# An expert layer of a two-block transformer in 18 steps for 24: lanes of 64, 32 and 32 slots, dealt from the experts' counts

## The chip, the cores and the metric

One core of a Trainium2 chip runs the whole program in one launch. The metric is the device time in microseconds of one execution, the median of several runs; lower is better.

## The reference, cut to what matters

Two transformer blocks over 512 tokens of 1024 features, all in f32. The first has two kinds of attention, and then a mixture of 32 experts in 4 groups of 8: a router takes the best group of each token and the best 2 experts in it, so 1024 token-expert pairs are computed:

```python
for g in range(N_GROUPS):
    a = jnp.einsum('td,edf->tef', t, w_gate[sl])
    u = jnp.einsum('td,edf->tef', t, w_up[sl])
    hid = jax.nn.silu(a) * u * combine[:, g, :, None]
    y = y + jnp.einsum('tef,efd->td', hid, w_down[sl])
```

An expert has w_gate and w_up (1024 x 256 each) and w_down (256 x 1024), 1 MB each. `combine` is zero but for a token's two experts. The second block (two more attentions, two dense FFNs of 4096) is not touched by the change.

## The kernel before, in words

Each engine has its own instruction stream, and the streams meet at semaphores. Tiles keep the features on the 128 partitions, tokens on the free axis, but for the expert layer, which works on gathered rows.

**The router.** After the first block's attention, TensorE computes the router's logits and turns the normed tokens, which ACT writes to a table in HBM (`tokens_normed`). DVE picks groups and experts (L3044 to L3066), TensorE counts for each token-expert pair its place among the pairs of that expert, and each expert's total (L1777 to L1786, group "rank"). From these DVE works out the position of each pair among all slots (L3079 to L3103: `whole` rounds, a scan sums the extra blocks, the positions are added up under the one-hot choice), splits it into step and slot (L3106, L3108), and builds one-hot matrices (L3117, L3121). TensorE multiplies them into a table of slots (L1793), and DVE writes from it the token of each slot, the row of its output and its weight (`slot_tok`, `slot_y`, `slot_w`, L3130 to L3135), and the experts of the extra blocks with a flag for used (`extra_exp`, L3137, L3138). DVE instructions that need the one ahead are joined by `link`, a semaphore that DVE waits for itself.

**The steps.** There are 24 steps of 128 slots in two halves (`HALF` = 64). Steps 0 to 15 in `COLUMN`'s numbering are fixed: the halves belong to experts 2c and 2c+1. Eight more steps take what goes over 64 in an expert, in blocks of 64 of one expert each; `COLUMN` puts them between the fixed ones, after steps 2, 4, 6, 8, 10, 11, 12 and 13. Step b does:

- POOL gathers the 128 token rows with an indirect DMA (L1248; three buffers), and slots without a token are left out;
- TensorE turns them (L1805, eight transposes, "moe_T"), DVE adds a shift on the way out of PSUM (L3146);
- `gate_up` (L1821, "moe_GU"): for each of 8 slices of features, one product for each half, with 64 columns of tokens as the stationary operand and 512 columns of that expert's w_gate and w_up moving. The two halves write to partitions 0 to 63 and 64 to 127 of one PSUM bank;
- ACT takes the silu (L2499), DVE multiplies with the other half and the slot's weight (L3160);
- `turn_hidden` (L1831) and `down` (L1847, "moe_D"): two transposes, then four products for each half, to two banks;
- ACT and DVE copy the banks out (L2189, L2710), POOL scatters the rows to `y_dram` (L1257).

TensorE's order (`moe_schedule`) is turn_hidden(b), gate_up(b+1), turn_tokens(b+2), down(b). A product in f32 shows as two records in the trace. L1805, L1831 have the full 128 columns as stationary operand, L1821 and L1847 have 64.

**The weights.** SP's queue issues all loads in the order of its code. Expert weights have five places (`ESLOTS`), one per half-step: half n goes to place n % 5. SP loads halves 0 and 1, then 2, 3, 4 during the end of the attention and the router; after gate_up(b) it loads w_gate and w_up of the halves that take these places (L1037, L1039), after down(b-1) w_down of theirs (L1044). A fixed half has an address known when the program is written. For an extra one SP reads the expert and the flag from `extra_exp` into registers (`value_load`), and the DMA is skipped where the flag is 0. Behind the layer, the next stage's weights (L1113) wait for the third last step's down products.

```python
            for b in range(STEPS - 1):
                sp.wait_ge(mm_done, done(G[("moe_GU", b)]))
                for n in range(2 * b + ESLOTS, min(2 * b + ESLOTS + 2, 2 * STEPS)):
                    load_gate_up(n)
```

Most of the rest of the program is TensorE's: the dense products of the two FFNs and the projections, as three products of split halves (L1425 to L1427).

Of the kernel before, what the change touches and what calls it, by code (L numbers as in the profile page):

```python
# [40 lines left out]
MAGIC = float(1.5 * 2 ** 23)  # L41
PI = 3.1415925
# [15 lines left out]
PAIRS = NE // 2  # L58
EXTRA = 8
STEPS = PAIRS + EXTRA  # L60


COLUMN = []
for _b in range(PAIRS):
    COLUMN.append(_b)
    if _b in (2, 4, 6, 8, 10, 11, 12, 13):
        COLUMN.append(PAIRS + len([c for c in COLUMN if c >= PAIRS]))
COLUMN += [PAIRS + n for n in range(len([c for c in COLUMN if c >= PAIRS]), EXTRA)]
ESLOTS = 5
TOKEN_BUFS = 3  # L70
# [269 lines left out]
def two_block_kernel(nc, a, out):  # L340

    G, W, W_LAST, W_VALUE = plan()
    with ExitStack() as ctx:
# [252 lines left out]
        r_all, r_log = rsmall(NT, 36), rsmall(NT, NE)  # L596
        r_mask, r_oh, r_pos = rsmall(NT, NE), rsmall(2, NT, NE), rsmall(NT, NE)
        r_sel, r_o1, r_o2 = rsmall(NT, 8), rsmall(NT, 8), rsmall(NT, 8)
        r_go, r_m, r_rank = rsmall(NT, 4), rsmall(8, NT), rsmall(8)
        r_shift, r_extra, r_cum, r_add, r_one = (rsmall(NE) for _ in range(5))  # L600
        add_table, slot_table, centred = rsmall(NE), rsmall(NE), rsmall(P)
        r_cmp = ar(r_off[0], 2 * EXTRA, NE, rows=1)
        r_off[0] += 2 * EXTRA * NE
# [7 lines left out]
        blk_id, r_be = (ar(r_off[0] + n * NBLK, NBLK, rows=1) for n in range(2))  # L611
        r_off[0] += 2 * NBLK
# [4 lines left out]
        extra_exp = sb("extra_experts", [1, 2, 2 * EXTRA], U32)  # L617
# [295 lines left out]
        def moe_slot(b, side):  # L913

            return (2 * b + side) % ESLOTS, (2 * b + side) // ESLOTS
# [18 lines left out]
        def _(sp):  # L934
# [89 lines left out]
            def expert_of(n):  # L1024

                c = COLUMN[n // 2]
                if c < PAIRS:
                    return 2 * c + n % 2, None
                b = 2 * (c - PAIRS) + n % 2
                sp.sem_inc(s_sp_go, 1)  # L1030
                e = sp.value_load(extra_exp[0:1, 0, b:b + 1], min_val=0, max_val=NE - 1)
                return e, sp.value_load(extra_exp[0:1, 1, b:b + 1], min_val=0, max_val=1)

            def load_gate_up(n):
                e, used = expert_of(n)
                dst = e_gate_up[n % ESLOTS]
                sp.dma_start(dst[:, 0:2048], expert_rows(a["w_gate"][0], e), cond=used)\  # L1037
                    .then_inc(s_egu[n % ESLOTS], 16)
                sp.dma_start(dst[:, 2048:4096], expert_rows(a["w_up"][0], e), cond=used)\  # L1039
                    .then_inc(s_egu[n % ESLOTS], 16)  # L1040

            def load_down(n):
                e, used = expert_of(n)
                sp.dma_start(e_down[n % ESLOTS], expert_rows(a["w_down"][0], e), cond=used)\  # L1044
                    .then_inc(s_edn[n % ESLOTS], 16)
# [6 lines left out]
            with nc.allow_non_contiguous_dma("narrow router weights"):  # L1052
                sp.dma_start(router_w[:, :, 0:4], kt(a["w_rg"][0])).then_inc(s_rw, 16)
                sp.dma_start(router_w[:, :, 4:36], kt(a["w_re"][0])).then_inc(s_rw, 16)
            load_gate_up(2)
            sp.wait_ge(mm_done, done(G[("out", 1)] + 3))
            load_gate_up(3)
            load_down(3)
# [33 lines left out]
            sp.wait_ge(mm_done, done(G["h_tok"] + 2 * NT - 1))  # L1092
            load_gate_up(4)
            sp.wait_ge(s_htok, 16 * NT)
            load_down(2)
            load_down(4)
            sp.wait_ge(s_bexp, 1)
            for b in range(STEPS - 1):
                sp.wait_ge(mm_done, done(G[("moe_GU", b)]))
                for n in range(2 * b + ESLOTS, min(2 * b + ESLOTS + 2, 2 * STEPS)):  # L1100
                    load_gate_up(n)
                if b:
                    sp.wait_ge(mm_done, done(G[("moe_D", b - 1)] + 1))
                    for n in range(2 * b - 2 + ESLOTS, min(2 * b + ESLOTS, 2 * STEPS)):
                        load_down(n)
# [6 lines left out]
            sp.wait_ge(mm_done, done(G[("moe_D", STEPS - 3)] + 1))  # L1112
# [56 lines left out]
        def _(pool):  # L1169
# [73 lines left out]
            def gather(b):  # L1243

                if b >= TOKEN_BUFS:
                    pool.wait_ge(mm_done, done(G[("moe_T", b - TOKEN_BUFS)] + 1))
                c = COLUMN[b]
                pool.indirect_dma_start(e_tok[b % TOKEN_BUFS], None, htok_dram,  # L1248
                                        bass.IndirectOffsetOnAxis(slot_tok[:, c:c + 1], 0), bounds_check=T - 1,
                                        oob_is_err=False).then_inc(s_gath[b % TOKEN_BUFS], 16)  # L1250

            def scatter(b):

                for n in range(2):
                    g_read(pool, G[("moe_D", b)] + n)
                c = COLUMN[b]
                pool.indirect_dma_start(y_dram, bass.IndirectOffsetOnAxis(slot_y[:, c:c + 1], 0),  # L1257
                                        e_out[b % 2], None, bounds_check=2 * T - 1,
                                        oob_is_err=False).then_inc(s_yst[b % 2], 16)
# [70 lines left out]
        def _(pe):  # L1330
# [477 lines left out]
            def gate_up(b):  # L1808
                g = G[("moe_GU", b)]
                weights = []  # L1810
                for side in range(2):
                    i, nth = moe_slot(b, side)
                    pe.wait_ge(s_egu[i], 32 * (nth + 1))
                    weights.append(e_gate_up[i].rearrange("p (g k n) -> p k g n", g=2, k=KD))
# [3 lines left out]
                for k in range(KD):  # L1818
                    for side in range(2):
# [14 lines left out]
            def down(b):  # L1834
                weights = []
                for side in range(2):
                    i, nth = moe_slot(b, side)
                    pe.wait_ge(s_edn[i], 16 * (nth + 1))
                    weights.append(e_down[i].rearrange("p (f d) -> p f d", f=2))
                g_read(pe, G[("moe_H", b)])  # L1840
                for n in range(2):
                    g = G[("moe_D", b)] + n
                    g_free(pe, g)
                    for f in range(2):
                        for side in range(2):
                            r = slice(HALF * side, HALF * side + HALF)
                            last = pe.matmul(psum(g)[r, :], e_hidT[:, b % 2, f, r],  # L1847
                                             weights[side][:, f, 512 * n:512 * n + 512], start=(f == 0), stop=(f == 1),
# [851 lines left out]
        def _(dve):  # L2700
# [306 lines left out]
            link(dve.memset(r_shift[:, :], -32.5 / P))  # L3007
# [19 lines left out]
            dve.tensor_scalar(add_table[:, :], iota[:, 0:NE], float(-HALF), float(PAIRS * P - HALF), ALU.mult, ALU.add)  # L3027
            link(dve.tensor_scalar(slot_table[:, :], iota[:, 0:NE], float(HALF), -63.5, ALU.mult, ALU.add))
# [48 lines left out]
            def whole(dst, src, scale):  # L3077
# [10 lines left out]
            link(dve.scalar_tensor_tensor(out=r_add[:, :], in0=r_cum[:, :], scalar=float(HALF), in1=add_table[:, :],  # L3088
                                          op0=ALU.mult, op1=ALU.add))
            link(dve.scalar_tensor_tensor(out=r_add[:, :], in0=r_extra[:, :], scalar=float(-HALF), in1=r_add[:, :],  # L3090
                                          op0=ALU.mult, op1=ALU.add))
            spread_add = r_add[:, :].unsqueeze(1).broadcast_to([P, NT, NE])
            link(dve.scalar_tensor_tensor(out=r_mask[:, :, :], in0=place, scalar=float(HALF), in1=spread_add,
                                          op0=ALU.is_ge, op1=ALU.mult))
            dve.tensor_tensor(r_pos[:, :, :], place, r_mask[:, :, :], ALU.add).then_inc(freed[g % BANKS], 1)
            g_read(dve, g)
            link(dve.tensor_tensor(r_pos[:, :, :], r_pos[:, :, :],
                                   slot_table[:, :].unsqueeze(1).broadcast_to([P, NT, NE]), ALU.add))
# [4 lines left out]
            link(dve.tensor_reduce(at_, both, AXX, ALU.add))  # L3103
            whole(r_step[:, :], at_, 1.0 / P)
# [14 lines left out]
            for k in range(2):  # L3119
# [4 lines left out]
            n = 2 * EXTRA  # L3124
            link(dve.tensor_tensor(r_cmp[0:1, :, :], blk_id[0:1, 0:n].unsqueeze(2).broadcast_to([1, n, NE]),
                                   r_cum[0:1, :].unsqueeze(1).broadcast_to([1, n, NE]), ALU.is_ge))
            link(dve.tensor_reduce(r_be[0:1, 0:n], r_cmp[0:1, :, :], AXX, ALU.add))
# [9 lines left out]
            link(dve.tensor_scalar(extra_exp[0:1, 0, :], r_be[0:1, 0:n], float(NE - 1), None, ALU.min))  # L3137
            dve.tensor_scalar(extra_exp[0:1, 1, :], r_be[0:1, 0:n], float(NE), None, ALU.is_lt).then_inc(s_bexp, 1)  # L3138
# [12 lines left out]
            def gate_up(b):  # L3151
                g = G[("moe_GU", b)]
                c = COLUMN[b]
# [3 lines left out]
                def by_row(v):  # L3157
# [3 lines left out]
                                         in0=by_row(psum(g)[:, FF:2 * FF]), scalar=slot_w[:, c:c + 1],  # L3161
# [6 lines left out]
            def down(b):  # L3168
# [3 lines left out]
                if b == STEPS - 4:  # L3172
                    c = COLUMN[STEPS - 1]
# [368 lines left out]
```

## Time and profile before

| | |
|---|---|
| median of 3 runs | 2032.26 us (2025.28 to 2032.86) |
| the profiled execution | 2028.45 us, its span 2026.4 us |
| mean granted TensorE clock | 0.983 |
| TensorE busy | 1950.7 us (96%) |
| DVE, ACT, POOL busy | 986.1, 662.0, 162.7 us |
| DMA over the span | 292.55 MB, mean 144 GB/s |
| the expert layer, first gate_up to last down | 477.3 to 770.2 us |

The profile is one execution. In its rows PE is TensorE's products, PEld its weight loads, SPq and POOLq the queues of engines that issue DMAs. Tile names are those of the program's memory, and several tiles share one name: `arena`, `weight_ring`, `hT` and `toeplitz_bias` hold expert weights here.

### The profile page before, as it was taken

What the parts mean: (1) busy time and instruction counts of PE and PEld (TensorE: products, weight loads), DVE (VectorE), ACT (ScalarE), POOL (GpSimd) and SP (SyncE); (2) the same over time, 40 slices, a digit from 0 to 9 for tenths busy, and PEclk for the clock granted to TensorE, in tenths of its full rate; (3) what the DMA queues carried; (4) which work ended last, traced back from release to release, by engine and by line L of the source; (5) the groups of instructions that cost most, each with busy time, mean ns of one, the idle gap of its engine ahead of it and who ended that gap; (6) DMA issues with size and microseconds to landing.
All of it is one profiled execution on the core that took longest, in us unless ns stands there. A gap on an engine that the chain in (4) does not pass through costs nothing.

```text
span 2026.4 us, 23969 instructions
## 1 busy us (share of the span) xinstructions
PE 1950.7 (96%) x9117; PEld 1353.6 (67%) x9117; DVE 986.1 (49%) x1865; ACT 662.0 (33%) x1238; POOL 162.7 (8%) x169
## 2 busy tenths in 40 slices
PE   7999899996999999988999999999999999999998
PEld 3478576673333334446888888888677888888886
DVE  6474545342122222584565555555256756555554
ACT  2572722241111112358432222232336633222222
POOL 1000000021111110204100000011000020000001
PEclk9999999997999999999999999999999999999999
DMA  9555134357999787110322322232440022232201
GB/s 320 191 141 189 61 130 161 143 184 281 418 397 361 287 328 264 42 42 1 120 88 83 104 105 83 103 105 92 165 156 1 1 84 83 89 119 83 90 35 42
DMA packets 104871, 292.55 MB, mean 144 GB/s; under 512 B 13445, under 2 KB 24403, under 8 KB 91712
## 3 DMA queue, kind: packets, MB, share of 16 engines
q1 hardware_dynamic: 92352, 266.60, 35.7%
q0 software_dynamic: 11408, 22.27, 3.5%
q10 hardware_dynamic: 1008, 2.29, 0.3%
q8 instruction: 68, 1.11, 0.2%
q14 instruction: 35, 0.29, 0.0%
HBM read 331.22 MB, written 24.69 MB: 176 GB/s over the span
## 4 chain that ended last, share of the span: by engine, by line
PE 87%; DVE 7%; DMA 2%; ACT 2%; issue 1%; ACTq 0%; DVEq 0%; SPq 0%; POOLq 0%
PE bank L1425 18%; PE bank L1427 17%; PE bank L1426 17%; PE bank L1821 8%; PE bank L1342 5%; PE bank L1847 4%; PE bank L1384 3%; PE bank L1410 2%; PE bank L1396 2%; PE bank L1877 1%; PE bank L1629 1%; PE bank L1805 1%; DVE top L3313 1%; PE bank L1416 1%; DVE hT L3314 1%
## 5 line engine op out<-in xcount | busy, mean ns | idle before, releaser
L3203 DVE TENSOR_TENSOR weights_low<-weight_ring,weights_high 128x1024 fp32r<-128x1024 f32 x128 | 159.1, 1243 | 264.5 <-ACT weights_high L2303 264.5
L1427 PE MATMUL bank<-hidden_high,weights_low 128*128 128x512 f32 x688 | 267.6, 389 | 0.0
L1425 PE MATMUL bank<-hidden_high,weights_high 128*128 128x512 f32 x624 | 242.7, 389 | 0.0
L1426 PE MATMUL bank<-hidden_low,weights_high 128*128 128x512 f32 x624 | 242.7, 389 | 0.0
L2303 ACT ACTIVATE weights_high<-weight_ring 128x1024 fp32r<-128x1024 f32 x128 | 135.6, 1059 | 321.1 <-PE bank L1427 321.1
L1425 PE MATMUL bank<-normed_high,weights_high 128*128 128x512 f32 x512 | 200.4, 392 | 0.2
L1426 PE MATMUL bank<-normed_low,weights_high 128*128 128x512 f32 x512 | 199.3, 389 | 0.0
L1427 PE MATMUL bank<-normed_high,weights_low 128*128 128x512 f32 x512 | 199.2, 389 | 0.0
L1821 PE MATMUL bank<-weight_ring,arena 128*64 128x512 f32 x464 | 171.3, 598 | 4.6 <-issue 2.7
L1427 PEld LDWEIGHTS bank<-hidden_high,weights_low 128*128 128x128 f32 x688 | 129.1, 188 | 26.7
L1426 PEld LDWEIGHTS bank<-hidden_low,weights_high 128*128 128x128 f32 x624 | 117.1, 188 | 24.4
L1425 PEld LDWEIGHTS bank<-hidden_high,weights_high 128*128 128x128 f32 x624 | 117.1, 188 | 24.4
L2189 ACT ACTIVATE arena<-bank 128x512 f32<-128x512 f32 (+7 forms) x222 | 99.0, 465 | 96.6 <-PE bank L1831 34.0
L1425 PEld LDWEIGHTS bank<-normed_high,weights_high 128*128 128x128 f32 x512 | 96.1, 188 | 22.3 <-DVE weights_low L3203 1.1
L1426 PEld LDWEIGHTS bank<-normed_low,weights_high 128*128 128x128 f32 x512 | 96.1, 188 | 20.2 <-issue 0.5
L1427 PEld LDWEIGHTS bank<-normed_high,weights_low 128*128 128x128 f32 x512 | 96.1, 188 | 20.0
L3160 DVE SCALAR_TENSOR_TENSOR arena<-bank,slot_weights,arena 128x256 f32<-128x256 f32 x24 | 16.0, 668 | 175.2 <-ACT arena L2499 175.2
L1183 POOL TENSOR_TENSOR chunk_mask<-small,probs_T 128x512 f32<-128x512 f32 x5 | 6.5, 1306 | 1174.9 <-ACT probs_T L2290 1174.9
L2782 DVE TENSOR_TENSOR xT<-bank,xT 128x512 f32<-128x512 f32 x144 | 93.0, 682 | 7.0 <-PE bank L1427 7.0
L2341 ACT ACTIVATE hidden_high<-scores 128x512 fp32r<-128x512 f32 x64 | 40.5, 633 | 171.0 <-DVE scores L3256 171.0
L1821 PEld LDWEIGHTS bank<-weight_ring,arena 128*64 128x64 f32 x464 | 52.0, 138 | 63.0 <-issue 63.0
L1342 PE MATMUL bank<-arena,weight_ring 128*128 128x512 f32 (+1 forms) x204 | 88.6, 587 | 0.0
(567 smaller groups left out, 3522.3 us busy)
## 6 DMA issues: line engine op xcount, KB each, us to landing
weight_ring<-in_w_up SPq DMA_DIRECT2D x16, 2048.0 KB, 8.7
weight_ring<-in_w_down SPq DMA_DIRECT2D x16, 2048.0 KB, 7.8
weight_ring<-in_w_gate SPq DMA_DIRECT2D x29, 1024.0 KB
weight_ring<-in_w_up SPq DMA_DIRECT2D x29, 1024.0 KB
weight_ring<-in_w_ada SPq DMA_DIRECT2D x12, 2048.0 KB, 12.9
weight_ring<-in_w_down SPq DMA_DIRECT2D x19, 1024.0 KB
hT<-in_w_down SPq DMA_DIRECT2D x19, 1024.0 KB
weight_ring<-in_w_in SPq DMA_DIRECT2D x7, 2048.0 KB, 14.5
```

The costliest lines, as they stand in the source:

```text
L1342: last = pe.matmul(dst, l, r, start=(n == 0), stop=(n == len(pairs) - 1))
L1384: pe.matmul(psum(g + hd)[:, 0:n], pair_q(kind, p, hd, qt), pair_k(kind, p, hd, n), start=True, stop=True).then_inc(mm_done, 1)
L1396: last = pe.transpose(psum(g)[:, at:at + P], unit_scores(kind, u, hd)[:, kt * P:kt * P + P], ident[:, :])
L1425: pe.matmul(dst, high, rhs_high, start=first, stop=False)
L1426: pe.matmul(dst, high, rhs_low, start=False, stop=False)
L1427: return pe.matmul(dst, low, rhs_high, start=False, stop=last)
L1821: last = pe.matmul(psum(g)[r, :].rearrange("p (g n) -> p g n", g=2), e_tokT[:, b % 2, k, r], weights[side][:, k, :, :], start=(k == 0), st ...
L1847: last = pe.matmul(psum(g)[r, :], e_hidT[:, b % 2, f, r], weights[side][:, f, 512 * n:512 * n + 512], start=(f == 0), stop=(f == 1), skip_ ...
L2189: act.activation(dst, psum(g)[:, :] if src is None else src, func, scale=scale)\
L2303: act.activation(piece_half(w_hi, ch, q), piece_of(ch, q), ACT.Copy).then_inc(s_whi, 1)
L2782: ins = dve.tensor_tensor(xT[:, j, :], psum(g)[:, :], xT[:, j, :], ALU.add)
L3203: dve.tensor_tensor(piece_half(w_lo, ch, q), piece_of(ch, q), piece_half(w_hi, ch, q).bitcast(F32), ALU.subtract).then_inc(s_wlo, 1)
```

## The change

The layer has 18 steps. Steps 0 and 1 are as before, halves of 64 for experts 0 to 3. The other 16 have three lanes: 64 slots (partitions 0 to 63), 32 (64 to 95) and 32 (96 to 127), each with weights of its own. What an expert has (for experts 0 to 3 what goes over 64) is split into blocks of 64, as many as its count over 64 rounded, and one block of 32 where the rest needs one. Blocks of 64 take the lanes of 64 in order; blocks of 32 take first the 16 lanes at 64, then those at 96; blocks of 64 beyond 16 take two lanes of 32. The positions get the arithmetic for that, the expert of each lane is computed in tables, and all lanes but the first four get their weights through registers, with a flag that skips a load. An entry, one lane of one step, has one of five places in turn, in the order 0, 1, 3, 4, 2.

```diff
-PAIRS = NE // 2
-EXTRA = 8
-STEPS = PAIRS + EXTRA
+FIXED = 4
+WIDE = 16
+STEPS = FIXED // 2 + WIDE
+ENTRIES = FIXED + 3 * WIDE
+LANES = ((0, 64), (64, 96), (96, 128))
 ESLOTS = 5
+EHOME = (0, 1, 3, 4, 2)
...
+        def moe_entries(b):
+            if b < FIXED // 2:
+                return tuple((2 * b + n, HALF * n, HALF * n + HALF) for n in range(2))
+            return tuple((FIXED + 3 * (b - FIXED // 2) + n, r0, r1) for n, (r0, r1) in enumerate(LANES))
+        def entry_home(n):
+            return EHOME[n % ESLOTS], n // ESLOTS
...
             def expert_of(n):
-                c = COLUMN[n // 2]
-                if c < PAIRS:
-                    return 2 * c + n % 2, None
-                b = 2 * (c - PAIRS) + n % 2
+                if n < FIXED:
+                    return n, None
+                q, lane = (n - FIXED) // 3, (n - FIXED) % 3
+                i = WIDE * lane + q
                 sp.sem_inc(s_sp_go, 1)
-                e = sp.value_load(extra_exp[0:1, 0, b:b + 1], min_val=0, max_val=NE - 1)
-                return e, sp.value_load(extra_exp[0:1, 1, b:b + 1], min_val=0, max_val=1)
+                e = sp.value_load(entry_exp[0:1, 0, i:i + 1], min_val=0, max_val=NE - 1)
+                if n < ESLOTS:
+                    return e, None
+                return e, sp.value_load(entry_exp[0:1, 1, i:i + 1], min_val=0, max_val=1)
...
             sp.wait_ge(mm_done, done(G["h_tok"] + 2 * NT - 1))
+            load_gate_up(3)
+            sp.wait_ge(s_htok, 16 * NT)
+            load_down(3)
+            sp.wait_ge(s_bexp, 1)
             load_gate_up(4)
-            sp.wait_ge(s_htok, 16 * NT)
-            load_down(2)
             load_down(4)
-            sp.wait_ge(s_bexp, 1)
             for b in range(STEPS - 1):
                 sp.wait_ge(mm_done, done(G[("moe_GU", b)]))
-                for n in range(2 * b + ESLOTS, min(2 * b + ESLOTS + 2, 2 * STEPS)):
-                    load_gate_up(n)
+                for n, _, _ in moe_entries(b):
+                    if n + ESLOTS < ENTRIES:
+                        load_gate_up(n + ESLOTS)
                 if b:
                     sp.wait_ge(mm_done, done(G[("moe_D", b - 1)] + 1))
...
                 for k in range(KD):
-                    for side in range(2):
-                        r = slice(HALF * side, HALF * side + HALF)
+                    for r, w_gu in weights:
                         last = pe.matmul(psum(g)[r, :].rearrange("p (g n) -> p g n", g=2), e_tokT[:, b % 2, k, r],
-                                         weights[side][:, k, :, :], start=(k == 0), stop=(k == KD - 1),
+                                         w_gu[:, k, :, :], start=(k == 0), stop=(k == KD - 1),
...
-            whole(r_extra[:, :], psum(g)[:, NT * NE:NT * NE + NE], 1.0 / HALF)
-            link(dve.tensor_tensor_scan(r_cum[:, :], r_one[:, :], r_extra[:, :], 0.0, ALU.mult, ALU.add))
+            link(dve.tensor_scalar(r_single[:, :], count, 16.0, 2.0 / HALF, ALU.add, ALU.mult))
+            whole(r_pairs[:, :], count, 1.0 / HALF)
+            whole(r_single[:, :], r_single[:, :], 1.0)
+            link(dve.scalar_tensor_tensor(out=r_single[:, :], in0=r_pairs[:, :], scalar=-2.0, in1=r_single[:, :],
+                                          op0=ALU.mult, op1=ALU.add))
+            dve.tensor_tensor_scan(r_cum_pairs[:, :], r_one[:, :], r_pairs[:, :], 0.0, ALU.mult, ALU.add)
+            link(dve.tensor_tensor_scan(r_cum_single[:, :], r_one[:, :], r_single[:, :], 0.0, ALU.mult, ALU.add))
...
+            x, kind, entry, move, even = (v[:, :] for v in (r_x, r_kind, r_entry, r_move, r_even))
+            dve.tensor_scalar(even, at_, 1.0 / 32, MAGIC_EVEN, ALU.mult, ALU.add)
+            link(dve.tensor_scalar(x, at_, 1.0 / 32, 0.5, ALU.mult, ALU.add))
+            link(dve.tensor_scalar(x, x, MAGIC, None, ALU.add))
...
+            link(dve.scalar_tensor_tensor(out=at_, in0=move, scalar=32.0, in1=at_, op0=ALU.mult, op1=ALU.add))
             whole(r_step[:, :], at_, 1.0 / P)
...
+            entries_at(0, blk_id[0:1, 0:WIDE], r_cum_pairs)
+            entries_at(WIDE, blk_id[0:1, 0:WIDE], r_cum_single)
             g = G["table"]
             dve.wait_ge(mm_done, done(g))
...
+            entries_at(2 * WIDE, blk_id[0:1, WIDE:2 * WIDE], r_cum_single)
...
+            entries_at(3 * WIDE, r_half[0:1, 0:WIDE], r_cum_pairs)
+            entries_at(4 * WIDE, r_half[0:1, WIDE:2 * WIDE], r_cum_pairs)
...
+            link(dve.tensor_scalar(entry_exp[0:1, 0, :], r_be[0:1, 0:n], float(NE - 1), None, ALU.min))
+            dve.tensor_scalar(entry_exp[0:1, 1, :], r_be[0:1, 0:n], float(NE), None, ALU.is_lt).then_inc(s_bexp, 1)
```

`entries_at` is two instructions over 16 x 32 elements, a comparison and a sum. `down` loops over the lanes as `gate_up` does. The next stage's weights (L1113) are loaded behind the second last step's down products. Nineteen instructions over [128, 8] stand between the sum of positions and `whole(r_step...)`, which move each position from its block to its lane.

## Rows read from the trace of the kernel before

**Rows 1.** The chain that ended last, shares of the span by engine.
```profile
PE 87%; DVE 7%; DMA 2%; ACT 2%; issue 1%; ACTq 0%; DVEq 0%; SPq 0%; POOLq 0%
```

**Rows 2.** Stretch; busy us (count) of five engines; clock, DMA share, GB/s.
```profile
489.00:573.00 84.00, 81.28 (x397) 30.23 (x395) 16.62 (x27) 8.58 (x19) 12.21 (x12) 1.00 1.01 413
573.00:765.00 192.00, 192.00 (x930) 68.94 (x926) 39.66 (x67) 22.45 (x49) 30.80 (x30) 1.00 0.88 338
...
537.00:549.00 12.00, 9.87 (x50) 4.19 (x52) 1.78 (x3) 0.38 (x1) 2.04 (x2) 1.00 1.02 422
```

**Rows 3.** The chain in order of time, expert layer's start: start us, us, what.
```profile
468.88 5.43 DMA arena<-tokens_normed,slot_tokens
...
477.31 8.51 PE bank L1821 x32
...
488.38 7.09 PE bank L1821 x32
```

**Rows 4.** Single lines: count, ns min/median/max, first and last start us.
```profile
L3160 DVE SCALAR_TENSOR_TENSOR arena<-bank,slot_weights,arena x24: 665/667/673, 486.3 to 762.6; 128x256 f32<-128x256 f32 x24
...
L1847 PE MATMUL bank<-hT,arena x152: 592/592/644, 508.4 to 769.6; 128*64 128x512 f32 x152
```

**Rows 5.** Timeline of one change of shape: start us, us, engine line op.
```profile
569.18 0.59 PE L1821 MATMUL bank<-toeplitz_bias,arena 128*64 128x512 f32 x1
569.18 0.14 PEld L1821 LDWEIGHTS bank<-toeplitz_bias,arena 128*64 128x64 f32 x1 [0.28 <-issue]
569.19 0.59 PE L1821 MATMUL bank<-weight_ring,arena 128*64 128x512 f32 x1
...
569.61 0.59 PE L1821 MATMUL bank<-toeplitz_bias,arena 128*64 128x512 f32 x1
...
570.14 0.86 PEld L1805 LDWEIGHTS bank<-ident,probs_T 128*128 128x128 f32 x8 [0.81 <-issue]
570.14 1.09 PE L1805 MATMUL bank<-ident,probs_T 128*128 128x128 f32 x8
...
571.16 0.64 PE L1847 MATMUL bank<-hT,arena 128*64 128x512 f32 x1
...
571.64 0.59 PE L1847 MATMUL bank<-hT,arena 128*64 128x512 f32 x1
```

**Rows 6.** Timeline of the router's dealing on DVE, and the first gather.
```profile
457.44 0.19 DVE L3079 TENSOR_SCALAR arena<-bank 128x32 f32<-128x32 f32 x1 [1.52 <-PE bank L1786]
...
460.47 0.17 DVE L3079 TENSOR_SCALAR arena<-arena 128x8 f32<-128x8 f32 x1
460.68 0.17 DVE L3080 TENSOR_SCALAR arena<-arena 128x8 f32<-128x8 f32 x1
...
468.88 1.10 POOL L1248 DMA_INDIRECT arena<-tokens_normed,slot_tokens  x1 [19.46 <-DVE slot_tokens L3131]
```

**Rows 7.** Timeline of SP: a static load, then a dealt and skipped one.
```profile
519.86 0.44 SPq L1039 DMA_DIRECT2D arena<-in_w_up  x1
521.80 0.11 SPq L1037 DMA_DIRECT2D weight_ring<-in_w_gate  x1
```

**Rows 8.** Timeline of TensorE: lanes of 32 columns in the first layer.
```profile
65.11 1.93 PE L1645 MATMUL bank<-hT,arena 128*32 128x512 f32 x16
```

**Rows 9.** Timeline of weight loads, then products, in the banded attention.
```profile
228.04 0.47 PEld L1396 LDWEIGHTS bank<-ident,arena 128*128 128x128 f32 x4
228.68 0.64 PEld L1416 LDWEIGHTS bank<-probs_T,arena 128*64 128x64 f32 x12 [0.17 <-issue]
...
228.15 0.60 PE L1396 MATMUL bank<-ident,arena 128*128 128x128 f32 x4
228.68 0.88 PE L1416 MATMUL bank<-probs_T,arena 128*64 128x128 f32 x12
```

**Rows 10.** A group of the expert layer: count, busy us, mean ns, idle.
```profile
L1805 PE MATMUL bank<-ident,probs_T 128*128 128x128 f32 x64 | 8.7, 279 | 0.0
```

**Rows 11.** DMA queues from 470 to 775 us: packets, MB, share.
```profile
q0 software_dynamic: 6768, 8.10, 7.6%
```

More of the change, by code:

```diff
@@ L594, in rsmall @@
             return v
-        r_all, r_log = rsmall(NT, 36), rsmall(NT, NE)
-        r_mask, r_oh, r_pos = rsmall(NT, NE), rsmall(2, NT, NE), rsmall(NT, NE)
+        r_all, r_chosen, r_log = rsmall(NT, 36), r_off[0], rsmall(NT, NE)
+        r_mask, r_spread, r_oh, r_pos = rsmall(NT, NE), r_off[0], rsmall(2, NT, NE), rsmall(NT, NE)
+        r_choice = r_off[0]
         r_sel, r_o1, r_o2 = rsmall(NT, 8), rsmall(NT, 8), rsmall(NT, 8)
         r_go, r_m, r_rank = rsmall(NT, 4), rsmall(8, NT), rsmall(8)
[L600 to L603, printed above, removed]
+        r_shift, r_pairs, r_single, r_at_pair, r_at_single, r_from, r_one = (rsmall(NE) for _ in range(7))
+        r_cum_pairs, r_cum_single = rsmall(NE), rsmall(NE)
+        pair_table, from_table, fixed_table, centred = rsmall(NE), rsmall(NE), rsmall(FIXED), rsmall(P)
+        r_fixed, r_fixed_add = rsmall(FIXED), rsmall(NT, FIXED)
+        r_x, r_kind, r_entry, r_move, r_even = (ar(r_choice + 2 * NT * n, 2 * NT) for n in range(5))
+        r_cmp = ar(r_off[0], WIDE, NE, rows=1)
+        r_off[0] += WIDE * NE
         r_tok, r_row = rsmall(2 * NT, P), rsmall(2 * NT, 2, STEPS)
@@ L610, in two_block_kernel @@
         tok_id = rsmall(NT)
-        blk_id, r_be = (ar(r_off[0] + n * NBLK, NBLK, rows=1) for n in range(2))
-        r_off[0] += 2 * NBLK
+        blk_id = ar(r_off[0], NBLK, rows=1)
+        r_off[0] += NBLK
+        r_be, r_half = ar(r_chosen, 5 * WIDE, rows=1), ar(r_chosen + 5 * WIDE, 33, rows=1)
         assert r_off[0] <= 15872
@@ L616, in two_block_kernel @@
         slot_w = sb("slot_weights", [P, STEPS])
[L617 removed]
+        entry_exp = ar(r_spread, 2, 3 * WIDE, rows=1).bitcast(U32)
         before = sb("strictly_before", [P, P])
@@ L1810, in gate_up @@
                 weights = []
-                for side in range(2):
-                    i, nth = moe_slot(b, side)
+                for n, r0, r1 in moe_entries(b):
+                    i, nth = entry_home(n)
                     pe.wait_ge(s_egu[i], 32 * (nth + 1))
-                    weights.append(e_gate_up[i].rearrange("p (g k n) -> p k g n", g=2, k=KD))
+                    weights.append((slice(r0, r1), e_gate_up[i].rearrange("p (g k n) -> p k g n", g=2, k=KD)))
                 for m in range(2):
@@ L1835, in down @@
                 weights = []
-                for side in range(2):
-                    i, nth = moe_slot(b, side)
+                for n, r0, r1 in moe_entries(b):
+                    i, nth = entry_home(n)
                     pe.wait_ge(s_edn[i], 16 * (nth + 1))
-                    weights.append(e_down[i].rearrange("p (f d) -> p f d", f=2))
+                    weights.append((slice(r0, r1), e_down[i].rearrange("p (f d) -> p f d", f=2)))
                 g_read(pe, G[("moe_H", b)])
@@ L1844, in down @@
                     for f in range(2):
-                        for side in range(2):
-                            r = slice(HALF * side, HALF * side + HALF)
+                        for r, w_d in weights:
                             last = pe.matmul(psum(g)[r, :], e_hidT[:, b % 2, f, r],
-                                             weights[side][:, f, 512 * n:512 * n + 512], start=(f == 0), stop=(f == 1),
+                                             w_d[:, f, 512 * n:512 * n + 512], start=(f == 0), stop=(f == 1),
                                              skip_group_check=True)
@@ L3006, in _ @@
             dve.memset(r_one[:, :], 1.0)
-            link(dve.memset(r_shift[:, :], -32.5 / P))
+            for v, fixed, others in ((r_shift, -(HALF + 0.5) / P, -0.5 / P), (pair_table, -31.5 - HALF, -31.5)):
+                dve.memset(v[:, 0:FIXED], fixed)
+                dve.memset(v[:, FIXED:NE], others)
+            dve.memset(from_table[:, FIXED:NE], 0.0)
+            link(dve.memset(from_table[:, 0:FIXED], float(HALF)))
             evac(G["router"] + 1, router_parts[1])
@@ L3092, in _ @@
-            spread_add = r_add[:, :].unsqueeze(1).broadcast_to([P, NT, NE])
-            link(dve.scalar_tensor_tensor(out=r_mask[:, :, :], in0=place, scalar=float(HALF), in1=spread_add,
-                                          op0=ALU.is_ge, op1=ALU.mult))
+            count = psum(g)[:, NT * NE:NT * NE + NE]
+            link(dve.tensor_scalar(r_single[:, :], count, 16.0, 2.0 / HALF, ALU.add, ALU.mult))
+            whole(r_pairs[:, :], count, 1.0 / HALF)
+            whole(r_single[:, :], r_single[:, :], 1.0)
@@ new lines, in _ @@
+            link(dve.tensor_tensor(r_at_single[:, :], r_cum_single[:, :], r_single[:, :], ALU.subtract))
+            dve.tensor_tensor(r_at_pair[:, :], r_cum_pairs[:, :], r_pairs[:, :], ALU.subtract)
+            link(dve.tensor_scalar(r_at_single[:, :], r_at_single[:, :], singles, 32.0, ALU.subtract, ALU.mult))
+            link(dve.scalar_tensor_tensor(out=r_at_pair[:, :], in0=r_at_pair[:, :], scalar=float(HALF),
+                                          in1=pair_table[:, :], op0=ALU.mult, op1=ALU.add))
@@ new lines, in _, with by_token @@
+            link(dve.tensor_tensor(r_at_single[:, :], r_at_single[:, :], r_from[:, :], ALU.subtract))
+            dve.tensor_tensor(r_fixed[:, :], fixed_table[:, :], r_at_pair[:, 0:FIXED], ALU.subtract)
+            link(dve.scalar_tensor_tensor(out=r_at_single[:, :], in0=r_at_single[:, :], scalar=-31.5,
+                                          in1=r_at_pair[:, :], op0=ALU.add, op1=ALU.subtract))
+            def by_token(v, n=NE):
+                return v.unsqueeze(1).broadcast_to([P, NT, n])
@@ L3095, in _ @@
+            dve.scalar_tensor_tensor(out=r_fixed_add[:, :, :], in0=place[:, :, 0:FIXED], scalar=float(HALF),
+                                     in1=by_token(r_fixed[:, :], FIXED), op0=ALU.is_lt, op1=ALU.mult)
+            link(dve.tensor_tensor(r_mask[:, :, :], place, by_token(r_from[:, :]), ALU.is_ge))
+            link(dve.tensor_tensor(r_mask[:, :, :], r_mask[:, :, :], by_token(r_at_single[:, :]), ALU.mult))
             dve.tensor_tensor(r_pos[:, :, :], place, r_mask[:, :, :], ALU.add).then_inc(freed[g % BANKS], 1)
```

97 lines of the change are left out of this document (57 added, 40 removed).

## The prediction

> **What bounds the kernel now.** The first view is the chain of work that ended last: TensorE holds 87% of it [rows 1], so what a change gives or takes has to show on TensorE, or on what makes it wait. The second is the table of busy time by stretch, over the expert layer [rows 2]: from 573 to 765 us TensorE is busy in all 192.00 us at a granted clock of 1.00 (the upper level, 2.4 GHz), with the DMA engines at 0.88. From 489 to 573 us the DMA engines stand at 1.01 and 413 GB/s, and TensorE loses 2.7 us of 84; 2.1 of them between 537 and 549. There the steps took their two fixed experts each. So the layer is bound by TensorE, and two new experts a step are about more than the DMA brings in a step's time.
>
> The third view is one step on the chain [rows 3]: 7.09 us of gate and up products (L1821, 32 records), about half as long for the down products (L1847, 16 records), the rest transposes. The 24 instructions of L3160 start at 486.3 to 762.6 [rows 4], so a step is 276.3/23 = 12.01 us. Within a step both 64-slot lanes run side by side: the records of two lanes share a start, and the next pair starts 0.43 us later, not 0.86 [rows 5].
>
> **How the lanes are filled.** Counting the choices that the reference's router makes for its inputs (1024 over 32 experts, 3 to 121 each; experts 0 to 3 have 36, 5, 51, 28), the new dealing uses the 4 fixed lanes, 14 of the 16 lanes of 64, the 16 first lanes of 32 and none of the 16 second ones: 34 expert loads. Before, it is 32 fixed lanes and 2 of 16 extra ones: 34 too. The traffic of weights is the same 34 x 3.15 MB (4 x 1024 x 256 x 3 bytes each), in 18 steps for 24.
>
> **What goes.** Six steps of 12.01 us on TensorE: -72.1 us.
>
> **The router is longer.** From the rank product to the slot table, DVE's chain is on the path: the first gather waits 19.46 us and ends with DVE's slot tokens [rows 6]. By the diff, the part up to the sum of positions goes from 10 to 24 instructions, and 19 on [128, 8] follow: 33 more. Small linked ones start 0.21 us apart [rows 6]. Nine of the 33 have no link behind them and can start under the one ahead, so I count them at half: 24 x 0.21 + 9 x 0.1 = 6 us. Bounds: 33 x 0.1 = 3 and 33 x 0.3 = 10 (the ten of before take 3.03 us with the wide ones among them [rows 6]). TensorE has nothing else there, so all of it is on the path.
>
> The expert tables move behind the slot table and grow by six instructions over 512 elements and some small ones. SP waits for them before it loads lane 4, which is first used in step 2, two steps later; and DVE's next work waits for the first gather, whose landing takes 5.43 us on the chain [rows 3]. Four more such instructions stand ahead of it, beside the table product; before it was two. Nothing for these, and one or two us if they outlast that cover.
>
> **SP.** Two register loads stand ahead of each dealt lane: the static issue at 519.86 ends at 520.30, the dealt one starts at 521.80, so 1.5 us. A skipped DMA then takes 0.11, a real one 0.44 [rows 7]. A wide step has three such lanes twice: 6 x 1.5 + 6 x 0.4 + 3 x 0.1 = 11.7 us of SP. That is less than any step time below, so I count nothing; were the steps at 11 us it would bind. The load of the next stage's weights (L1113) is issued one step before the end and not two, and first used behind the layer's final sums. POOL's gather and scatter fall to 18 and 17 and stay beside.
>
> **The three lanes.** This decides. If 64, 32 and 32 columns run side by side, a wide step stays 12 us on TensorE. The trace has no 64 next to a 32. It has lanes of equal width: 16 records of 32 columns in four lanes take 1.93 us, four abreast, where 16 starts 0.43 apart would take 6.9 [rows 8]. And it has changes of shape, 64 to 128 columns and back [rows 5], and in the banded attention 128 to 64 [rows 9]. Within one shape the next weights are loaded ahead (weight load at 228.04, its product at 228.15 [rows 9]). At the change the load starts only with its product (228.68 and 228.68; 570.14 and 570.14). So the array lets one shape end before it takes the next. The price of a change [rows 5]: 569.61 to 570.14 is 0.53, which is 0.10 over the pitch of 0.43. On the way back, eight transposes take 1.09 us, the last of them 0.28 [rows 5, 10], so their starts are 0.12 apart and the next would fall at 571.07; the products start at 571.16, and their second pair is 0.05 late: 0.14. I take the mean, 0.12.
>
> The Trainium skill, "TensorEngine Tiling (Array Packing)", Tiling Modes (Key Properties), says that a change of tiling mode, other than a change of tile, drains the engine, and lists 64 and 32 columns as different modes. The trace agrees for 64 against 128; no run here shows 64 against 32. By this rule the sum is the one that follows.
>
> If the lane of 64 can't run beside those of 32, each of the 12 products of a wide step (8 for gate and up, 4 for down; two records a lane) goes from 0.86 us to 2 x (0.86 + 0.12) = 1.96: +1.10. Per wide step 13.2, a step of 25.2 us; 16 of them +211 us. The two steps of two 64-lanes stay. Loads of 6.3 MB in 25.2 us are 250 GB/s, under the 413 that the DMA does, so nothing hides behind or sticks out. Bounds: at 0.10 a change it is 204; if the lanes change with each record and not with each product, 24 x (0.43 + 0.24) = 16.1 a step and 257; with 0.3 a change (0.16 of a record's overhang past its pitch and 0.14 of weight load, both uncovered [rows 5]) by product 16 x 12 x 1.46 = 280.
>
> **Sum.** 2028.45 of the profiled execution - 72 + 211 + 6 = 2173. The median of the runs shown is 3.8 higher; I say 2175.
>
> **The rivals.**
> *All three lanes abreast, DMA the bound: 2009.* For it: equal lanes run abreast in any number, and nothing shown forbids unequal ones in separate columns; the widths at each change in [rows 5, 9] share columns, so the change may be a conflict and no mode. The Trainium skill, "TensorE: Matmul & The Clock Gate", Part 3 (The mechanism), has tiles chosen by column masks and run together, without a word on equal widths; no run here shows that for unequal ones. Then -72 isn't all kept: a wide step with two loads needs 6.29 MB and 0.45 of tokens (8.10 MB on the software queue [rows 11], over 18 steps), which at 413 GB/s is 16.3 us against 12. Up to the gate and up products of step 15 the DMA has to bring 27 loads less two down parts, 82.8 MB, and 6.8 of tokens: 217 us, starting some 3 us after the first gate and up product. Two steps of 12 and the last one's 15 us follow: 259. Now it is 770.2 - 485.8 = 284 [rows 3, 4]. So -25 + 6 = -19, or 2009; between 1995 (fewer bytes late, the queue at 422 [rows 2]) and 2020 (SP's 11.7 us letting the queue run dry).
> *Abreast and the loads hidden: 2028 - 72 + 6 = 1962.* Against it: 29 loads after the start are 91 MB, 221 us at 413 GB/s, and the layer would have 212.
> *Abreast, but each change costs its 0.12 without a serial lane:* 12 x 0.24 = 2.9 us a step goes under the DMA's 4.3: the first rival again. Only with that and the upper bound of the router would it be no change, some 2025.
> *The dealing does not fit, lanes are lost:* 14 pairs of 16 and 16 singles of 32 fit.
>
> **Chances.** Serial lanes 0.62 (2150 to 2250), abreast with the DMA the bound 0.29, abreast and hidden 0.04, no change 0.05. The weight loads that are never ahead at a change speak for the first; that no row has the pair of widths keeps the second high. The likeliest case alone is 2150 to 2250; to leave out less than 2 in 10 the range goes down to 2000, into the second. A measurement tells about 0.5% here, 10 us: faster 0.32, the same 0.05, slower 0.63.
>
> **What would show it.** Serial: the 64-lane records of L1821's successor start alone and those of the 32-lanes about 0.5 or 0.95 us after them, weight loads start with their products, a wide step's gate and up stretch is 15 us and not 7, DMA share falls to about 0.6, TensorE stays busy. Abreast: triples share a start, TensorE waits for weights about 4 us a step, DMA at 1.0 through the layer. The router: the first gather 6 us later after the rank product. The forecast is wrong if the triples start together.

## The result, and the profile after

The changed kernel takes 2164.61 us (median of 4 runs, 2162.15 to 2167.78), the kernel before 2032.01 us beside it: a ratio of 1.066, 95% interval 1.063 to 1.069. It is slower, and 2175 was forecast. The profiled execution takes 2162.15 us with a span of 2160.4, against 2028.45 and 2026.4: +133.7 us. The ratios here and below count fast runs only: two runs of the kernel with two lanes of 64 (2198.77 and 10737.57 us) and one of the kernel before (3683.97 us) were slow and stay out of them.

The page after: busy time of TensorE, three lines of the 40 slices (granted clock, DMA share, GB/s; a slice is 54 us), and the chain by engine and line.

```profile
PE 2083.6 (96%) x9153; PEld 1333.8 (62%) x9153; DVE 982.3 (45%) x1891; ACT 654.7 (30%) x1220; POOL 151.3 (7%) x157
...
PEclk9999999979999999999999999999999999999999
DMA  9546043357667774350022323222343012323211
GB/s 332 186 96 231 25 174 141 131 208 285 257 265 280 283 278 179 117 195 19 22 78 78 116 80 110 85 105 90 117 159 112 1 40 78 114 82 107 88 39 39
...
PE 88%; DVE 7%; DMA 2%; ACT 1%; issue 1%; ACTq 0%; DVEq 0%; SPq 0%; POOLq 0%
```

TensorE's share of the chain goes from 87% [rows 1] to 88%, and its busy time grows from 1950.7 to 2083.6 us: 132.9 of the 133.7. So the loss is work or occupation of TensorE, not waiting. The stretch table says the same of the layer (columns as in [rows 2]):

```profile
498.00:899.00 401.00, 401.00 (x1318) 81.68 (x1314) 41.45 (x70) 22.87 (x50) 30.83 (x30) 1.00 0.61 241
```

TensorE is busy in all 401 us at a granted clock of 1.00, and the DMA engines stand at 0.61 and 241 GB/s, where [rows 2] had 1.01 and 0.88. In the chain of waits (start, us, what) one sees which steps grew. L1838 is gate and up (L1821 before), L1863 down (L1847 before).

```profile
467.80 3.62 PE bank L1811 x16
...
472.86 4.04 DMA arena<-tokens_normed,slot_tokens
476.95 1.98 PE bank L1823 x8
...
479.90 9.31 PE bank L1838 x32
...
491.77 7.09 PE bank L1838 x32
...
503.83 15.88 PE bank L1838 x48
```

The first two steps, of two lanes of 64, still take 7.09 us for gate and up [rows 3]. The first wide step takes 15.88, and so do the others. The timeline of one wide step shows why: first the weight loads, then the products (start, us, engine, line, stationary shape, count, idle before).

```profile
600.25 0.19 PEld L1838 LDWEIGHTS bank<-arena 128*64 128x64 f32 x2 [0.17 <-issue]
601.26 0.11 PEld L1838 LDWEIGHTS bank<-weight_ring,arena 128*32 128x32 f32 x1 [0.81 <-issue]
...
602.24 0.19 PEld L1838 LDWEIGHTS bank<-arena 128*64 128x64 f32 x2 [0.84 <-issue]
...
600.26 1.07 PE L1838 MATMUL bank<-arena 128*64 128x512 f32 x2
601.26 0.62 PE L1838 MATMUL bank<-weight_ring,arena 128*32 128x512 f32 x1
601.26 0.62 PE L1838 MATMUL bank<-toeplitz_bias,arena 128*32 128x512 f32 x1
601.71 0.59 PE L1838 MATMUL bank<-weight_ring,arena 128*32 128x512 f32 x1
601.72 0.59 PE L1838 MATMUL bank<-toeplitz_bias,arena 128*32 128x512 f32 x1
602.24 1.07 PE L1838 MATMUL bank<-arena 128*64 128x512 f32 x2
```

The two lanes of 32 share their starts (601.26 and 601.26), so they lie abreast. The lane of 64 has TensorE to itself from 600.26 to 601.26, and the next round starts at 602.24. No weight load runs ahead of a change of width: the first load of each width starts with its product (601.26 and 601.26, 602.24 and 602.24). So a product of all lanes takes 1.985 us on average (15.88/8), where it took 0.86 [rows 5].

The router's part: the rank product's reader on DVE, and the first gather on POOL with its wait.

```profile
455.56 0.19 DVE L3105 TENSOR_SCALAR arena<-bank 128x32 f32<-128x32 f32 x1 [1.52 <-PE bank L1804]
...
472.86 1.10 POOL L1267 DMA_INDIRECT arena<-tokens_normed,slot_tokens  x1 [25.22 <-DVE slot_tokens L3195]
```

From the one to the other it is 17.30 us; before it was 468.88 - 457.44 = 11.44 [rows 6].

### The profile page after: what moved, and what is told of

It reads as the page before. It is cut to its first block, busy times and chain, and to the rows that moved or that the text cites. A ratio compares the mean times of both kernels' runs of the same rounds, so it can differ in the third digit from the quotient of the medians.

```text
span 2160.4 us, 24592 instructions
## 1 busy us (share of the span) xinstructions
PE 2083.6 (96%) x9153; PEld 1333.8 (62%) x9153; DVE 982.3 (45%) x1891; ACT 654.7 (30%) x1220; POOL 151.3 (7%) x157
## 4 chain that ended last, share of the span: by engine, by line
PE 88%; DVE 7%; DMA 2%; ACT 1%; issue 1%; ACTq 0%; DVEq 0%; SPq 0%; POOLq 0%
PE bank L1443 17%; PE bank L1445 16%; PE bank L1444 16%; PE bank L1838 13%; PE bank L1863 6%; PE bank L1360 5%; PE bank L1402 3%; PE bank L1428 2%; PE bank L1414 1%; PE bank L1893 1%; DVE top L3388 1%; PE bank L1647 1%; DVE hT L3389 1%; PE bank L1434 1%; PE bank L1823 1%
## 5 line engine op out<-in xcount | busy, mean ns | idle before, releaser
L1838 PE MATMUL bank<-weight_ring,arena 128*64 128x512 f32 (+1 forms) x496 | 226.1, 613 | 1.9 <-DVE arena L3222 1.9
L1838 PEld LDWEIGHTS bank<-weight_ring,arena 128*64 128x64 f32 (+1 forms) x496 | 37.8, 119 | 136.8 <-issue 136.8
L1838 PE MATMUL bank<-arena 128*32 128x512 f32 (+1 forms) x176 | 93.5, 621 | 0.0
L2515 ACT ACTIVATE arena<-bank 128x256 f32<-128x256 f32 x18 | 6.9, 385 | 279.0 <-PE bank L1838 279.0
```

## The experiments

The theory: 64 and 32 columns can't be in the array together, so the lane of 64 stands alone (the first part of the loss), and each change of width costs some 0.13 us (the second). The rivals: three lanes cost more than two whatever their widths; SP's register reads or the dealing hold the steps up; the weight bytes do. Ratios are to the kernel before, run on the same chip, with 95% intervals.

**Four lanes of 32 in the changed kernel.** The same weights and slots; the lane of 64 is computed as two products of 32 columns.

```diff
-weights.append((slice(r0, r1), e_gate_up[i]...))
+weights += [(slice(r, r + 32), w) for r in range(r0, r1, 32)]      # w = e_gate_up[i]...; down likewise
```

> The changed kernel, but every lane of 64 in gate_up and down is two lanes of 32 columns with the same weights, so all stationary operands of the layer are 32 wide; the result is the same computation. Width theory (unequal widths exclude each other, number and place of lanes do not matter): four abreast, the gate and up stretch falls from 15.9 to about 7.1 us, TensorE could do a step in 12 us, and then the DMA is the bound at about 16 us a step with 413 GB/s: 2000 to 2012 us, faster than the kernel before. Lane theory (only two streams of full products run abreast, whatever their width): two pairs in turn, 2160 us or more.

Measured: 2030.39 us (11 runs), ratio 1.0008 (0.9999 to 1.0017). With four products for three in each slice, the kernel is 134 us faster than the changed one: it is the widths, and not the number of lanes. The time is 18 us over the upper end of the expectation, in part because the weights are now late (what the profile has over 2009 is added up under "The rivals" below):

```profile
548.59 9.79 PE bank L1839 x64
...
577.99 5.00 issue
582.99 9.69 PE bank L1839 x64
...
612.74 5.06 issue
617.79 9.32 PE bank L1839 x64
```

These are rows of its chain of waits. In the 5 us of "issue" TensorE does nothing while the DMA engines are full (share 1.01 from 612.74 to 617.78); that these are waits for weights, the run with fewer bytes below shows. From 548.59 to 705.62, nine steps take 157.03 us, 17.45 each, and the DMA moves 62.81 MB, 6.98 a step, at 400 GB/s:

```profile
548.00:706.00 158.00, 122.65 (x958) 41.69 (x962) 22.38 (x36) 12.29 (x27) 18.27 (x18) 0.89 0.99 400
```

**The kernel before, with 64, 32 and 32.** The reverse: its second half as two products of 32 columns of the same weights, nothing else changed.

```diff
-for side in range(2):
-    r = slice(HALF * side, HALF * side + HALF)
+for side, r0, r1 in ((0, 0, 64), (1, 64, 96), (1, 96, 128)):
+    r = slice(r0, r1)
```

> The kernel before (24 steps, old router, old loads), only the second half of each step is computed as two lanes of 32 columns with the same weights; same computation. Width theory: each of 12 products a step goes from 0.86 to 1.985 us, 13.5 us a step, 24 steps: +325, so 2357 us. Lane theory (a third stream): slow as well, by 0.86 a product at least, 2280 or more. If the loss of the changed kernel came from its loads, registers or router: 2032.

Measured: 2342.83 us (4 runs), ratio 1.1548 (1.1526 to 1.1571). Its timeline has the pattern of the changed kernel: 64 alone for 1.00 us, the pair of 32 for 0.99.

```profile
572.99 1.07 PE L1821 MATMUL bank<-weight_ring,arena 128*64 128x512 f32 x2
573.99 1.05 PE L1821 MATMUL bank<-toeplitz_bias,arena 128*32 128x512 f32 x4
574.98 1.07 PE L1821 MATMUL bank<-weight_ring,arena 128*64 128x512 f32 x2
```

A step goes from 12.01 to 24.92 us, with the dealing, SP and the router untouched. It grows by 12.91 us where 13.5 was expected, so the time is 14 us under the forecast: 13.5 counts two changes for each of 12 products, 24, and there are 22; the rest of the difference stays open. So dealing, loads and router are not the cause, and with the run above, which keeps them and has four lanes, it is the mixture of widths.

**The kernel before, with four lanes of 32.** Both halves split.

```diff
+for side, r0, r1 in ((0, 0, 32), (0, 32, 64), (1, 64, 96), (1, 96, 128)):
```

> The kernel before, both halves computed as two lanes of 32 columns each with the same weights. Width theory: no unequal widths, four abreast: 2032 within 5 us. Lane theory (more than two streams): as slow as with 64, 32, 32 or slower, 2280 to 2450.

Measured: 2029.57 us (10 runs), ratio 0.9997 (0.9986 to 1.0009); a step is 12.06 us. Twice the number of products at half the width costs nothing measurable: all four start within 0.01 us.

```profile
574.35 0.62 PE L1821 MATMUL bank<-arena 128*32 128x512 f32 x2
574.36 0.62 PE L1821 MATMUL bank<-weight_ring,arena 128*32 128x512 f32 x2
574.80 0.60 PE L1821 MATMUL bank<-arena 128*32 128x512 f32 x2
```

**Products of one width together.** The changed kernel, with all of a group's products of the lane of 64 first and then those of 32: 22 changes of width a step become 4.

```diff
-for k in range(KD):
-    for r, w_gu in weights:
+for k, r, w_gu in sorted(((k, *w) for k in range(KD) for w in weights),
+                         key=lambda v: (v[1].stop - v[1].start != HALF, v[0])):
```

> The changed kernel with the order of the products changed: in gate_up all eight of the lane of 64 and then those of the two lanes of 32, in down the same within each bank. Changes between 64 and 32 in a wide step go from 22 to 4. Width theory with a price of 0.13 to 0.14 us for each change: 18 x 0.1375 x 16 = 40 us less, 2124 us, still serial. If the lanes wait for each other for another reason and a change as such is free: 2160 as before.

Measured: 2133.29 us (4 runs), ratio 1.0513 (1.0497 to 1.0530), 31 us under the changed kernel. A step takes 22.79 us for 25.21 (starts of gate and up 592.36 and 615.15): 2.42 us for 18 changes, 0.134 each. In the chain the gate and up stretch is down from 15.88 to 14.00:

```profile
592.36 14.00 PE bank L1839 x48
607.38 7.40 PE bank L1865 x24
615.15 14.00 PE bank L1839 x48
```

The layer (end of the first gate and up to end of the last down) gains 38.7 us, the 40 expected; 8 come back outside it, in code that is not changed (1241.1 us from the next stage's first product to the end, 1233.2 in the changed kernel; more of that below). The larger part of the loss is the two widths taking turns, and it is left when they are grouped.

**Two lanes of 64.** The changed kernel's wide steps as 64 and 64: a block of 32 uses the first half of a second lane of 64. The third lane, empty for these inputs, is left out, so this is no general kernel.

```diff
-LANES = ((0, 64), (64, 96), (96, 128))
+LANES = ((0, 64), (64, 128))
```

> The changed kernel with two lanes of 64 in each wide step: the blocks of 64 as before, the blocks of 32 in the first half of a second lane of 64; the third lane, empty for these inputs, is left out. All products of a step have one width. Theory 'width': lanes of one width lie abreast, gate/up takes 7.0 us as in the kernel before, and the step is set by the weight bytes, as with lanes of 32: 2015 to 2035 us. If it were the number of dealt lanes of 32 that cost, or the dealing itself, and not that 64 and 32 columns alternate, it would stay at 2100 us or above.

Measured: 2026.63 us (median of 10 runs; 2024.8 of the eight that the ratio counts), ratio 0.9974 (0.9959 to 0.9989). The 18 steps and their dealing are as in the changed kernel, and so is the length of the router; the widths are equal, and the 138 us are gone. Here too the layer is bound by the weights. Three stretches of it, a wait for weights, the products behind it, and the ones after these:

```profile
613.04:616.46 3.42, 0.00 (x1) 0.03 (x1) 0.43 (x1) 0.38 (x1) 1.82 (x2) 1.00 1.01 417
616.47:619.87 3.40, 3.40 (x9) 1.20 (x11) 0.00 (x0) 0.00 (x0) 0.20 (x1) 0.51 1.02 423
619.87:625.20 5.33, 5.33 (x27) 1.96 (x23) 0.00 (x0) 0.00 (x0) 0.00 (x0) 0.99 1.02 418
```

After a wait of 3.42 us the granted clock is 0.51 (the lower level, 1.2 GHz) for 3.40 us, and gate and up take 8.78 us for 7.02. As the DMA engines are at 1.02 all the while, a full clock would here only make the next wait longer; that is argued, and no run tests it.

**The experts as constants.** The version with four lanes of 32, without any register read.

```diff
-e = sp.value_load(entry_exp[0:1, 0, i:i + 1], ...)
-return e, sp.value_load(entry_exp[0:1, 1, i:i + 1], ...)
+return DEALT[i], None
```

> The version with every lane computed as lanes of 32 columns, with the experts of the dealt lanes as constants for these inputs: SP reads no register, no weight load is conditional, and the loads of an empty lane are a few bytes. It leaves out the dealing as the source of the weights. Theory 'bytes': the DMA engines set the step, the bytes are the same, so the time is within 10 us of 2030. Rival 'registers': SP's register reads are what delays the loads; without them the stretch from 505 to 715 us shrinks and the time falls by 20 us or more, to 2010 or below.

Measured: 2029.99 us (10 runs), ratio 1.0003 (0.9985 to 1.0021). SP's reads don't set the time, and the stretch doesn't shrink; it has the same DMA share:

```profile
548.00:706.00 158.00, 122.52 (x956) 41.95 (x954) 23.26 (x39) 12.29 (x27) 18.28 (x18) 0.89 0.99 394
```

**Fewer weight bytes.** Four lanes of 32, and from the sixth lane on an eighth of w_up.

```diff
-sp.dma_start(dst[:, 2048:4096], expert_rows(a["w_up"][0], e), cond=used)
+cols = 2048 if n < ESLOTS else 256
+sp.dma_start(dst[:, 2048:2048 + cols], expert_rows(a["w_up"][0], e)[:, 0:cols], cond=used)
```

> The changed kernel with every lane computed as lanes of 32 columns (the version that took 2030 us), with the up weights cut: from the sixth lane on only 256 of the 2048 up columns of a partition are loaded, so a dealt lane brings 0.92 MB less of its 3.1 MB. It leaves out the loading of most up weights. Theory 'bytes': in that version the steps of 17.45 us are set by the DMA engines (share 0.94 to 1.02 at 404 GB/s), so with some 30% fewer bytes a step costs 12.0 to 12.5 us of TensorE work, the TensorE clock stays at 1.00 because no wait for weights is left, and the expert stretch shrinks from 271 to about 218 us: 1960 to 1985 us. Rival 'latency': what a step waits for is not the bytes but the path of one load (SP's turn, issue, landing) after its home came free; then fewer bytes shorten a step by less than 2 us, and the time stays above 2005 us.

Measured: 1975.66 us (4 runs), ratio 0.9741 (0.9717 to 0.9766). Between the profiles (2032.2 and 1969.7 us of span) the layer, from the end of the first gate and up to the end of the last down, falls from 271.2 to 221.7 us; another 11.0 us come from unchanged code behind it (1247.8 and 1236.8 us). In its chain the waits shrink from 5 us to some 1.3, and gate and up stay at 7.07:

```profile
603.72 1.27 issue
604.98 7.07 PE bank L1840 x64
...
617.02 1.44 issue
618.46 7.07 PE bank L1840 x64
```

```profile
564.00:671.00 107.00, 96.36 (x850) 35.03 (x848) 19.95 (x33) 10.91 (x24) 16.20 (x16) 1.00 0.99 380
```

The second fence is its stretch table: the DMA is still full. From 565.55 to 659.11 seven steps take 13.37 us and 5.07 MB each; that is some 1 us over the expectation's 12.0 to 12.5, as not all waits are gone. 1.91 MB less a step gives 4.1 us less, so the bytes set the step, and the waits of about 1.3 us do not lower the granted clock.

**The next stage's weights a step earlier.** In the version with two lanes of 64, the tail from the end of the last down (759.30) to the next stage is 22.3 us, 16.84 before. (The 27 us of the expectation start at the end of the second-last down, 754.63; from there it is 21.5 in the kernel before.) SP issues the next stage's first weights (1792 and 288 KB) after the second-last down, and the two expert outputs 8 us behind them. In the chain, the scatter between the two takes 6.35 us:

```profile
756.25 6.35 DMA expert_outputs<-scores,slot_choices
...
781.58 1.52 PE bank L1893 x3
```

Another order of the five places lets SP issue these weights a step earlier, as before.

```diff
-EHOME = (0, 1, 3, 4, 2)
+EHOME = (1, 3, 0, 4, 2)      # entries 1 and 2 also change places at the start
-sp.wait_ge(mm_done, done(G[("moe_D", STEPS - 2)] + 1))
+sp.wait_ge(mm_done, done(G[("moe_D", STEPS - 3)] + 1))
```

> The version with two lanes of 64 in a wide step, with the five weight homes dealt in another order, so that the next stage's first weights (1.1 MB) can be loaded one step earlier, behind the second-last but one down instead of the second-last, as in the kernel before. If the 27 us from the last down to the next stage (16.84 before) come from these loads meeting the loads of the two expert outputs, that stretch shrinks by 5 to 9 us and the time falls from 2027 to 2016 to 2023 us. If the two loads only follow TensorE's lower clock or a later scatter, the time stays within 3 us of 2027.

(The loads are 2.1 MB, not the 1.1 of the expectation.) Measured: 2019.65 us (6 runs), ratio 0.9937 (0.9918 to 0.9956). In the chain, the scatter's transfer takes 2.64 us for 6.35, and the next stage starts at 775.31:

```profile
755.71 2.64 DMA expert_outputs<-scores,slot_choices
758.36 0.37 SPq L1135
758.78 7.62 DMA toeplitz_bias<-expert_outputs
...
775.31 27.70 PE bank L1890 x64
```

The tail is 16.6 us from the end of the last down (758.76), as in the kernel before; that is 5.7 of the 7.4 us between the two profiles. Of the kernels that load all the weights this is the fastest, for these inputs: the idea of 18 steps is worth 0.6% if the widths are equal.

## Why the prediction was right

Milestones of the two profiled executions, in order; the parts add up to +134.0, the difference of the spans.

| part | forecast | measured |
|---|---|---|
| up to the rank product's reader | 0 | -1.9 |
| from there to the first gather | +6 | +5.9 |
| gather to the first gate and up | 0 | -1.4 |
| first gate and up to the last down's end | -72 + 211 = +139 | 292.9 to 431.3: +138.5 |
| last down to the next stage | 0 | -0.9 |
| the rest, not changed | 0 | -6.2 |

**Serial lanes.** Right in mechanism and size. Each wide product was put at 1.96 us with 0.12 for a change; it takes 1.985. Starts of one width are 0.429 us apart (575.60 to 581.60 in the kernel before, 14 of them), so two for each of the two widths are 1.716; that leaves 0.134 a change, and grouping gave 0.134 too. Two small errors cancel here: the price was 0.12, and 24 changes a step were counted where there are 22 (15 in gate and up, 7 in down), 2.9 us a step either way. A wide step was forecast at 25.2 us and takes 25.21 (gate and up starts 600.26 and 625.47). The Trainium skill, "TensorEngine Tiling (Array Packing)", Tiling Modes (Key Properties), has TensorE drain when the tiling mode changes and not when only the tile does. The trace agrees, here for widths in columns that do not overlap: they start in turn (600.26, 601.26, 602.24), while four equal tiles start together (574.35, 574.36).

**The signs.** The 64-lane starts alone, the 32s come 1.00 us later (about 0.95 was given), loads start with their products, gate and up take 15.88 us for 15, DMA share is 0.61 for 0.6, the first gather comes 5.9 us later for 6. All the named signs of the serial case came, and none of the rival's.

**What was costed at nothing.** SP: no wait of TensorE but one of 1.40 us for a down weight, at the end, and constants for registers change nothing even where a step is 17 us. The expert tables: the last instruction on them runs from 477.85 to 478.03, and DVE's next work, on the gathered tokens, starts at 478.17. The cover held, with little to spare. The load of the next stage's weights one step later cost nothing here: the scatter took 6.97 us for 3.33, but from the second-last down's end to the last one's it is 9.7 us for 4.7, which covers that. In the versions with steps of 12 us at the end it cost 6 us. So this zero was right for the likeliest case only.

**The rivals.** "Abreast" is false for these widths, and its sum can be tried on equal ones: 2009 was forecast for it, the profiled run of four lanes of 32 took 2033.98. Against the forecast its layer took 271.2 us for 259, as a step brings 6.98 MB and not 6.74, and at 400 GB/s in the middle, not 413, with 288 in the first 24 us, when loads waited for the five places (12 us); the tail took 22.4 for 16.84 (6 us); the rest 1247.8 for 1239.4 at a lower granted clock (8 us); all ahead of it, the router included, 5 for 6. 2009 + 12 + 6 + 8 - 1 = 2034. "Abreast and hidden" falls with this: at 34 expert loads in 18 steps the DMA binds.

**What was not foreseen.** The changed kernel's profile is 11 us under the forecast's sum of 2173, and 6.2 of that is in unchanged code after the layer. Its granted clock is higher in places: the 100 us that begin 700 us after the next stage's first product stand at 0.95 in the changed kernel, and at 0.91 before. In the other versions this code took between 1236.8 and 1247.8 us. What decides when it falls there was not tried and stays open.

## What to carry to other kernels

Give products that are to lie side by side in the array one width, even if a lane is half empty or a product must be split: for 64 and 32 columns in f32, the widths tried here, four lanes of 32 cost the same as two of 64, and 64 beside two of 32 cost more than twice as much. When steps are cut, work out the bytes a step then needs at the rate that a full stretch of the trace shows: here TensorE was the bound of 24 steps and the DMA is the bound of 18, so 72 us saved on TensorE were worth 11 to 13 in the best version. Where no row shows a pair of shapes together, the weight loads do tell: a load that starts only with its product, at the changes between 64 and 128 columns, was a sign that held for this one too.

## What the hardware showed beside

- Widths exclude each other even where their columns don't overlap, and weights for the other width aren't loaded ahead; a change costs 0.134 us.
- After waits of 3.4 and 5.0 us the next products ran at the lower clock level (0.51 for 3.40 us, 0.50 for 4.21 us); after waits of some 1.3 us the clock stayed at 1.00.
- The transfer of a scatter, 2.64 us, took 6.35 beside the load of 1792 and 288 KB that was issued 1.6 us ahead of it: a load placed late delays what comes after it, and not only itself.
